# One Mamba-2 and attention block, then two layers with a Fourier mixer: Fourier weights folded once a layer, a bank for each Fourier group, and other orders of the first `v` unit, the output units and the scan's first masks

## What is computed

```python
def fourier_mix(u, w_f, b_f):                       # u: 256 x 512, in 4 groups of 128
    f = jnp.fft.fft(ug, axis=3, norm='ortho')
    f = jnp.fft.fft(f, axis=1, norm='ortho').real
    y = jnp.einsum('bsgc,gcd->bsgd', f, w_f)        # w_f: 128 x 128 for each group
    return y.reshape(B, S, FOURIER_WIDTH) + b_f
...
h = layer_norm(x, ln_in_g, ln_in_b)
for l in range(2):
    q, k, v, u = split(h @ w_in[l])
    o = diff_attention(q, k, v, lam, lam_init, subln_g)   # 8 heads, two softmaxes each
    m = concatenate([o, fourier_mix(u, w_f[l], b_f[l])])
    h = layer_norm(ALPHA * h + m @ w_o[l], ...)
    h = layer_norm(ALPHA * h + swiglu(h, w_gu[l], w_down[l]), ...)
```

## Time and profile before

| what | value |
|---|---|
| median of 3 runs | 970.16 us (969.46 to 970.74) |
| the profiled execution | 971.1 us, of it 969.3 us from the first to the last instruction |
| TensorE busy | 929.6 us, 96% |
| VectorE, ScalarE, GpSimd busy | 619.5, 475.4, 128.1 us |
| mean granted clock of TensorE | 0.986 of 2.4 GHz |
| chain that ended last | 82% TensorE, 7% VectorE, 4% ScalarE, 4% issue, 2% GpSimd |
| weight loads | 134 of 1 MB, 4.8 us each from issue to landing |
| parameter loads, Fourier weights | 1 MB in 4.8 us, 256 KB in 6.3 us |

### The profile page before, as it was taken

One profiled execution on the slowest core, in us unless ns is written; L12 is line 12 of the kernel. 1 busy time (PEld: TensorE's weight loads), 2 busy tenths in 40 slices (PEclk: granted clock), 3 DMA queues, 4 the chain that ended last, 5 costly groups with the idle time before them and its releaser, 6 DMA issues.

```text
span 969.3 us, 13483 instructions
## 1 busy us (share of the span) xinstructions
PE 929.6 (96%) x4974; PEld 782.1 (81%) x4974; DVE 619.5 (64%) x1073; ACT 475.4 (49%) x762; POOL 128.1 (13%) x100
## 2 busy tenths in 40 slices
PE   9999899999998979999999999998998999999996
PEld 6999678889887858877788888876976788888885
DVE  3798787766767685665865455557485675545545
ACT  6755656556685434763253343424475254434330
POOL 5542864202000010001100000000000100000001
PEclk9999899999999989999999999999999999999999
DMA  8655222473533127231475545444432237555521
GB/s 313 249 180 173 104 88 88 137 260 128 215 110 138 58 88 290 81 118 47 153 265 184 182 175 211 174 173 167 149 131 87 88 130 248 186 179 203 183 87 44
DMA packets 22235, 151.77 MB, mean 157 GB/s; under 512 B 2592, under 2 KB 2976, under 8 KB 4256
## 3 DMA queue, kind: packets, MB, share of 16 engines
q1 hardware_dynamic: 20160, 142.62, 41.2%
q10 hardware_dynamic: 2016, 8.34, 2.3%
HBM read 149.90 MB, written 1.05 MB: 156 GB/s over the span
## 4 chain that ended last, share of the span: by engine, by line
PE 82%; DVE 7%; ACT 4%; issue 4%; POOL 2%; DMA 1%; POOLq 0%; DVEq 0%; ACTq 0%; SPq 0%
PE ps L492 15%; PE ps L498 15%; PE ps L494 15%; PE ps L1077 5%; PE ps L523 3%; PE ps L527 3%; PE ps L525 3%; PE ps L543 2%; ACT whi L1247 2%; PE ps L1094 2%; PE ps L766 1%; PE ps L768 1%; PE ps L767 1%; PE ps L808 1%; DVE wlo L1705 1%
## 5 line engine op out<-in xcount | busy, mean ns | idle before, releaser
L1247 ACT CAST whi<-raw 128x2048 fp32r<-128x2048 f32 x127 | 241.8, 1912 | 142.3 <-PE ps L498 127.5
L1705 DVE TENSOR_TENSOR wlo<-raw,whi 128x1024 fp32r<-128x1024 f32 x127 | 166.3, 1310 | 160.0 <-ACT whi L1247 159.8
L492 PE MATMUL ps<-whi,ahi 128*128 128x512 f32 (+2 forms) x448 | 174.5, 390 | 0.2
L494 PE MATMUL ps<-wlo,ahi 128*128 128x512 f32 (+2 forms) x448 | 173.0, 386 | 0.0
L498 PE MATMUL ps<-whi,alo 128*128 128x512 f32 (+2 forms) x448 | 172.0, 387 | 0.0
L1711 DVE TENSOR_TENSOR wlo<-raw,whi 128x1024 fp32r<-128x1024 f32 x106 | 129.1, 1218 | 0.0
L492 PEld LDWEIGHTS ps<-whi,ahi 128*128 128x128 f32 x448 | 85.1, 190 | 17.3 <-issue 1.0
L498 PEld LDWEIGHTS ps<-whi,alo 128*128 128x128 f32 x448 | 84.9, 190 | 16.7
L494 PEld LDWEIGHTS ps<-wlo,ahi 128*128 128x128 f32 x448 | 85.2, 190 | 16.3
L492 PE MATMUL ps<-whi,bhi 128*128 128x512 f32 x206 | 82.4, 400 | 1.5 <-issue 1.5
L494 PE MATMUL ps<-wlo,bhi 128*128 128x512 f32 x206 | 80.3, 390 | 0.0
(11 more groups left out here) (286 smaller groups left out, 1747.8 us busy)
## 6 DMA issues: line engine op xcount, KB each, us to landing
raw<-in_wstream SPq DMA_DIRECT2D x134, 1024.0 KB, 4.8
par<-in_params ACTq DMA_DIRECT2D x5, 1024.0 KB, 4.8
tab<-in_tables ACTq DMA_DIRECT2D x1, 1354.0 KB, 7.8
res<-in_x SPq DMA_DIRECT2D x2, 512.0 KB, 4.6
out<-res SPq DMA_DIRECT2D x4, 256.0 KB, 2.1
par<-in_params ACTq DMA_DIRECT2D x1, 512.0 KB, 3.7
arena<-in_wf ACTq DMA_DIRECT2D x2, 256.0 KB, 6.3
arena<-in_wsmall ACTq DMA_DIRECT2D x1, 256.0 KB, 8.5
```

The lines of the kernel that those rows point to most:

```text
L492: pe.matmul(banks[b][:, 0:cw], h_, wh[:, i, c], start=st, stop=False, skip_group_check=True)
L494: pe.matmul(banks[b][:, 0:cw], h_, wl[:, i, c], start=False, stop=False, skip_group_check=True)
L1247: act.copy(whi[:, u % SPL, :], raw[:, u % RAW, :]).then_inc(w_hi, 1)
L1705: dve.tensor_tensor(wlo[:, u % SPL, c], raw[:, u % RAW, c], whi[:, u % SPL, c].bitcast(F32), ALU.subtract).then_inc(w_lo_v, 1)
```

## The change

- **Fold.** The table of the channels and `w_f` are multiplied once a layer: `cos_c` and `nsin_c` by all four groups' `w_f` (`wfs`), two matmuls of 512 columns to `X[0]` and `X[1]`, which ScalarE copies to `cw`. `fy` becomes two matmuls from `pqr` by `cw`, and `f` with its copy goes. `wfs` is loaded earlier: ahead of the first norm, and for the second layer in the first one's feed-forward stage.
- **Norm wait.** `v_products` does `vu` 0 on tile 0, then two busy matmuls, the turn of tile 1, the fold, `vu` 0 on tile 1, and `vu` 1 on both. VectorE's split of `vu` 1 moves behind the second tile's low parts. Two busy matmuls also stand ahead of the turn of tile 0 in the first layer.
- **A bank per group.** `FB = [G[0], G[1], X[0], X[1]]` replaces the `TP` fills; `pqr` has two buffers; the order is `F_ORDER`, one `pq` ahead of each `fy`. Groups 2 and 3 wait until all scores are read.
- **Output units.** In the stages of `w_o` the second half of the columns goes to `X[t]` (`acc_bank`), so that `w_o` 2 can start before the heads' values in `G[2]`, `G[3]` are read. Units 2 and 3 run as half products, the first one ahead of the last group and the last head's values; the turn of `od` stands behind both.
- **`subln`.** The gain moves from a multiplication of `od` to the two writes behind the turn (`halves_hi`, `halves_lo` with a column of `vec`), four pieces of 256 each where there were two of 512. Between the two tiles' multiplications VectorE splits unit `gu` 0.
- **Scan.** `mixw` of heads 0 to 3 moves ahead of `split.until(("z", 1))`.
- **Start.** Tile 0 of `x` is turned once it is normalised, instead of both together.

```diff
+F_ORDER = [("pq", 0), ("pq", 1), ("fy", 0), ("pq", 2), ("fy", 1), ("pq", 3), ("fy", 2), ("fy", 3)]
+F_END = {6: 2, 7: 4, 8: 6, 9: 7, 10: 8}
...
+        FB = [G[0], G[1], X[0], X[1]]
+        def acc_bank(n, t, b):
+            return X[t] if n in (2, 4) and b == 1 else G[2 * b + t]
...
-            pe.wait_ge(xn_done, T)
-            for j in range(4):
-                turn_pair(("x", j), xn, 2 * j * P)
+            for t in range(T):
+                pe.wait_ge(xn_done, t + 1)
...
             o_half(2, 1, 1)
+            keep_busy(X[0], 2)
             turn_tile_when(("h", 0), 0)
...
             for l in range(DEPTH):
-                lead_units([("vu", l, 0), ("vu", l, 1)], ("h", l), [[G[2], G[3]]], 1 + 2 * l)
+                pe.wait_ge(acc_read, 4 * (1 + 2 * l) + 2)
+                v_products(0, 0)
+                keep_busy(X[0], 2)
+                turn_tile_when(("h", l), 1)
+                pe.wait_ge(wf_in, 16 * (l + 1))
+                for q, name in enumerate(("cos_c", "nsin_c")):
+                    pe.matmul(X[q], const(name), wfs, start=True, stop=True).then_inc(f_fold, 1)
+                v_products(0, 1).then_inc(w_used, 1)
+                v_products(1, 0).then_inc(lead_t0, 1)
+                v_products(1, 1).then_inc(w_used, 1)
...
-                    elif kind == "f":
-                        wait_emptied(pe, FILL["pq", l, g])
-                        pe.matmul(bank[:, 0:S], const("cos_c"), pqr[:, 0:S], start=True, stop=False,
-                                  skip_group_check=True)
-                        mm = pe.matmul(bank[:, 0:S], const("nsin_c"), pqr[:, S:2 * S], start=False,
-                                       stop=True, skip_group_check=True)
                     else:
-                        pe.wait_ge(wf_in, 16 * (l + 1))
-                        wait_emptied(pe, FILL["f", l, g])
-                        mm = pe.matmul(bank[:, 0:S], wfs[:, g, :], ftr, start=True, stop=True,
-                                       skip_group_check=True)
-                    mm.then_inc(tp_full, 1)
+                        pe.wait_ge(f_copied, NG * l + copied_count(g))
+                        for q in range(2):
+                            mm = pe.matmul(bank[:, 0:S], cw[:, q, g * GD:(g + 1) * GD],
+                                           pqr[:, g % 2, q * S:(q + 1) * S], start=(q == 0), stop=(q == 1),
+                                           skip_group_check=True)
+                    mm.then_inc(f_full, 1)
...
                 for kind, g in fourier_steps(NH + 1):
                     fourier(kind, g)
+                w_o_half(2, 0, 0)
+                for kind, g in fourier_steps(NH + 2):
+                    fourier(kind, g)
+                diff_pv(NH - 1)
+                w_o_half(2, 1, 0)
+                for t in range(T):
+                    w_o_half(2, t, 1)
+                for b in range(2):
+                    for t in range(T):
+                        w_o_half(3, t, b)
...
+            for h in range(4):
+                mixw(h)
             split.until(("z", 1))
             for p in range(PAIRS):
-                mixw(2 * p)
-                mixw(2 * p + 1)
+                if p >= 2:
+                    mixw(2 * p)
+                    mixw(2 * p + 1)
...
-                    fourier_lo(2 + t)
                 for t in range(T):
+                    if t == 1:
+                        split.until(("gu", l, 0, 0), 0)
                     o_ = od[:, t, :].rearrange("p (h w) -> p h w", w=VD)
-                    sg = subg[:, l * VD:(l + 1) * VD].unsqueeze(1).to_broadcast([P, NH, VD])
                     dve.wait_ge(do_rs, T * l + t + 1)
-                    link(dve.tensor_tensor(
+                    dve.tensor_tensor(
                         o_, o_, ors[:, NH * t:NH * t + NH].unsqueeze(2).to_broadcast([P, NH, VD]),
-                        ALU.mult))
-                    dve.tensor_tensor(o_, o_, sg, ALU.mult).then_inc(do_done, 1)
+                        ALU.mult).then_inc(do_done, 1)
                 for j in range(2):
-                    halves_lo(("do", l, j), bhi, blo, 2 * j)
+                    halves_lo(("do", l, j), bhi, blo, 2 * j, ("subln", 2 * l))
```

## The result

| what | before | after |
|---|---|---|
| median of the runs | 970.45 us (969.46 to 970.74) | 954.37 us (952.71 to 956.23) |
| ratio after to before | | 0.9836, 95% interval 0.9825 to 0.9848 |
| profiled execution, first to last instruction | 969.3 us | 950.9 us |
| TensorE busy | 929.6 us | 922.6 us |
| mean granted clock of the profiled execution | 0.986 | 0.998 |

The change makes the kernel 1.6% faster. (970.45 us is the median of four runs of before; the prediction had 970.16, of three.) The direction and the range of the prediction (951 to 963) held; the single number, 957.4, was 3.0 us too high, and the time lies just outside the interval that was held most likely (955 to 960), near rival A (954.0).

A forecast was written before the change was run, and what follows sets the result against it. TensorE, with its waits and their clock, was taken to bound the kernel. Fourier and output 10.2, norms 2.9 and 1.4, scan 1.7 make 16.2 us, less 3.4 for the clock: 970.2 - 12.8 = 957.4 us, range 951 to 963.

The forecast's parts named there:

- rival A: Clock holds at both `w_o` 0 waits and in the first norm: 954.0 us, to 951 if scan gives 5; chance 0.27.
- What bounds the kernel: Whole kernel: TensorE busy 929.6 of 969.3 us, so only less TensorE work or fewer waits, with their clock effect, help.
- The Fourier and output stretch: From `pq` 0 to `w_o` 0: removed work, waits and breaks less a new wait, 5.1 us a layer, 10.2 in two.
- thin cover of 0.3 us: At the turn of `od`: VectorE's multiplication of tile 1 ends at 451.1, TensorE arrives at 451.4.
- The norm waits: At the layer norms: earlier transposes and filled waits save 2.9 us in the first layer, 1.4 in the second.
- The list at the end of the prediction: Signs to check in the profile, among them `qk` 0 starting 9 us, not 11.9, after the norm's transposes.
- The scan: At `cum_rows(4)`: masks ahead of splits start its rows 3.4 us earlier; less one low-clock stretch, 1.7 us gained.
- The clock: At both `w_o` 0 waits and the first norm: two drops out of three, costing 3.4 us.
- B: Clock drops at all three places, 959.1 us, or scan gives nothing and `od` comes late, 961; chance 0.20.
- C: Fourier stretch: ScalarE's copies still stand in front of each `fy`, 3.6 us a layer stay, 964.6 us; chance 0.04.
- D: Weight stream: `vu` 1's raw buffer freed some 8 us later delays `qk` 1 and later loads, 973 us; chance 0.04.
- wrong if casts wait for loads in the `qk` units: In the `qk` units: weight casts waiting for loads would show the prediction wrong.

The follow-up runs named there:

- e9: Kernel before the change with one of the two `f` matmuls of each Fourier group left out; 970.16 us, ratio to before 0.9997.
- e4: Changed kernel with fold and banks kept, but each group's `fy` straight behind its own `pq`; 967.91 us, ratio to before 0.9972.
- e10: Changed kernel with a third `fy` matmul added in each Fourier group, same result; 958.8 us, ratio to before 0.9886.
- e3: Changed kernel with VectorE's split of `vu` 1 back ahead of the last half's addition, both layers; 959.11 us, ratio to before 0.9895.
- e1: Changed kernel with the scan's four mask multiplications back behind the weight splits; 955.67 us, ratio to before 0.9852.
- e6: Changed kernel with one busy matmul behind the turns of `od`, inside the wait for `w_o` 0; 956.4 us, ratio to before 0.9842.
- e12: Changed kernel with two busy matmuls inside the scan's 2.54 us wait ahead of the fifth pair's rows; 953.41 us, ratio to before 0.9830.
- e5: Changed kernel without the busy matmuls of the norm waits; 957.09 us, ratio to before 0.9867.
- e2: Changed kernel with VectorE's four splits in the scan's loop moved behind the third pair of a group; 951.19 us, ratio to before 0.9803.
- e8: Changed kernel with later scan splits, `od` turned ahead of `w_o` 3's last half, `gu` 0's split behind `od`'s low parts; 949.68 us.
- e11: Changed kernel with later scan splits, earlier turn of `od`, and `gu` 0's split between tile 1's multiplication and `od`'s low parts; 948.43 us.

## Why the prediction came out as it did

**What bounds the kernel: right.** TensorE was the engine, and its waits and clock were where the time lay.

**The Fourier and output stretch: the total right, its parts not.** 5.1 us a layer were predicted, 5.2 measured twice. The walk from `pq` 0 gave 28.8 us to `w_o` 0, the trace 28.75. The turns of `od` had just the thin cover of 0.3 us that was worked out: VectorE's multiplication of tile 1 ends at 444.68 and TensorE arrives at 444.98. The new wait is 1.40 us against 1.8. What was wrong is the split of the sum in removed work (1.8), removed waits (3.6) and breaks (1.5) as if each were a gain of its own. e9 shows that removed matmul work alone gave 0.5 of 1.8 a layer. e4 shows that the fold and the new banks, with each `fy` straight behind its `pq`, make the stretch 1.5 us longer than before. So the gain hangs on the order, and with it the saved work counts in full (e10). No run has the fold with the old `TP` banks, or the new banks without the fold: what the banks, the order and the missing copy give each is not separated. That the three terms, wrong as single gains, add up to the measured 5.2 is not luck, since they are together the walk from `pq` 0 to `w_o` 0, and the walk was right.

**The norm waits: right in size and by place.** From the first turn of norm 1 to `qk` 0 the gain is 3.2 us against 2.9, in the second norm 1.4 against 1.4. The transposes of tile 1 started 2.3 us earlier against the turn of tile 0, as worked out. The list at the end of the prediction says that `qk` 0 starts 9 us after the norm's transposes; that was a slip, the walk itself gives 370.9 - 359.7 = 11.2, and the trace 11.1. What the place of the split is worth is shown by e3: 2.3 us and the clock behind it in the first norm, and, against my expectation for e3, also 1.5 in the second.

**The scan: the walk right, the price wrong.** The masks were done at 104.7 (predicted 105.0), three splits took until 113.3 (113.5), `cum_rows(4)` started at 116.36 (116.7) behind a wait of 2.54 (2.9). The failed step is "it starts those rows at 116.7 instead of 120.08, 3.4 us": the 120.08 of before already held the cost of its 6.8 us of low clock, and the walk stopped at this row, so that the two later waits (0.78 and 0.22) were left out. At equal clock the edit gives 0.7 us (e1 against e6), where 1.7 stood in the sum: this term was 1.0 us too large.

The rule of the Trainium skill on the shared port (SBUF — State Buffer, Who interferes with whom), that the two engines exclude each other for a whole instruction, stood beside this walk. The trace agrees: a VectorE split takes 2.9 us beside GpSimd's work and 1.2 alone.

**The clock: wrong, and the largest part of the 3.0 us.** The prediction took two drops out of three, 3.4 us, at the two waits for `w_o` 0 and in the first norm. Neither happened. In eight profiles (the changed kernel, e1 to e5, e10, e12) the 1.4 us wait for `w_o` 0 stands twice, and in none of the 16 places did the clock fall. In the ten profiles that have the busy matmuls and the split in its new place it did not fall in the first norm either. The drops came where no question had been put: behind the scan's wait of 2.54 us in five of the seven profiles that have it (one or two stretches of 3.4 us), and behind the old 1.8 us wait at L972 (L950 of before) in 13 of the 14 profiles, all but that of the changed kernel. The trace of before had shown this: the prediction's rows of the clock leave out two low stretches, one at this wait and one at the turn of tile 0 in norm 1, behind a wait of 2.22 us:

```profile
313.10:316.50 3.40, 3.34 (x17) 3.31 (x18) 3.26 (x13) 1.87 (x7) 0.00 (x0) 0.52 0.70 284
350.70:354.10 3.40, 3.40 (x13) 3.00 (x14) 3.33 (x6) 1.17 (x2) 0.00 (x0) 0.51 0.00 0
```

The second is gone with the change, where two busy matmuls leave 0.48 us of that wait. The size was wrong too: against the changed kernel's profile a low stretch of 3.4 us cost 0.4 to 1.0 us at L972, 0.7 to 0.9 in the scan and 1.2 to 1.5 in the norm, not 1.7, since part of it lies over waits. The changed kernel's own executions say the same: 950.9 us at a mean clock of 0.998 and 954.4 at 0.991, 3.5 us for some 13 us of low clock, four stretches, as an estimate from the two means.

The Trainium skill (TensorE: Matmul & The Clock Gate, Part 4: PE-mode transpose) says that transposes don't count as a busy TensorE in the same way. By that rule the 0.8 us of transposes and the 1.4 us of wait ahead of `w_o` 0 are 2.2 us that don't count, nearly as long as the scan's 2.54, and no drop followed in 16 places. They don't refute the rule, but it misled as a forecast.

**Luck in the sum.** Without the clock's 3.4 us the sum is 16.2 us, and the medians differ by 16.1 (970.45 - 954.37). That is closer than the terms deserve: the scan's was 1.0 too large, and the medians of both kernels hold low stretches in the scan and at L972 that no term weighed against each other.

**The rivals.** A (the clock holds in all three places, 954.0, chance 0.27) is what happened at these places, and its time is within 0.4 us of the median. B's thin cover at the turn held. C did not occur. D was the least clear: freeing `vu` 1's buffer later did make ScalarE's casts wait for loads, but TensorE did not feel it. ScalarE of the changed kernel:

```profile
369.11 1.90 ACT L1292 CAST whi<-raw 128x2048 fp32r<-128x2048 f32 x1 [6.75 <-DMA raw<-in_wstream]
371.60 1.92 ACT L1292 CAST whi<-raw 128x2048 fp32r<-128x2048 f32 x1 [0.58 <-DMA raw<-in_wstream]
```

Before had one such wait at this place, of 1.39 us. The second layer has the same two (5.05 and 0.73 us), where before had none. TensorE's next wait is at 379.88 and is 0.68 us, as before. The mark "wrong if casts wait for loads in the `qk` units" was too strict.

**Still open.** Why a wait of 1.8 us at L972 drops the clock in nearly every profile and 0.8 of transposes with a wait of 1.4 never does was not separated. Several shorter waits lie close together around L972; whether these are what matters was not tried.

## What to carry to other kernels

Before counting removed work as a gain, ask who sets the pace at that place: if a bank or a copy does, most of the work is free there, and it takes a new order to make it count. When two starts are compared across a change, take the cost of the clock out of both, and follow the walk to the point where all shifted waits have been met again. A split, a copy or a cast that fills a gap needs its input to be there when the gap opens; an idle time in the row of one engine does not show that.

## What the runs showed of the hardware that was not expected

- Whether a wait drops the clock differs between executions of the same order: behind the scan's 2.54 us wait there were 0, 3.4 or 6.8 us at 1.2 GHz. With the wait filled (e12) or cut to 0.56 (e2, e8, e11) there was none in these four profiles.
- Six busy matmuls at three places of the norm waits, whose results nothing reads, are worth 2.7 us of the median (e5, four executions of each).
- A VectorE weight split of 1.2 us took 2.9 where GpSimd worked too, and two splits of GpSimd's took 6.7 us there instead of 4.8 (changed kernel, between 104.65 and 113.34 us).
